# Expert-choice routing: token numbers and gates by fp32r products, scatter matrices at other places

## The reference

```python
def expert_choice_ffn(h, router_w, w_gate, w_up, w_down):
    cap = EC_CAPACITY * n // N_EXPERTS            # 64 latent or 32 context tokens per expert
    aff = jax.nn.softmax((h @ router_w).astype(F32), axis=-1)
    gate, idx = lax.top_k(jnp.swapaxes(aff, 1, 2), cap)
    xe = jax.vmap(lambda hb, ib: hb[ib])(h, idx)
    a = jnp.einsum('becd,edf->becf', xe, w_gate)
    u = jnp.einsum('becd,edf->becf', xe, w_up)
    ye = jnp.einsum('becf,efd->becd', jax.nn.silu(a) * u, w_down) * gate[..., None].astype(h.dtype)
    return ...zeros((n, D)).at[ib.reshape(-1)].add(yb.reshape(-1, D))
```

## Time and profile before

| | us |
|---|---|
| median of 3 runs | 2724.34 (2723.0 to 2728.15) |
| the profiled execution | 2721.45 |
| its span, first to last instruction | 2719.7 |
| mean granted TensorE clock | 0.97 of 2.4 GHz |

### The profile page before, as it was taken

One profiled execution on the slowest core, in us unless ns is written; L12 is line 12 of the kernel. 1 busy time (PEld: TensorE's weight loads), 2 busy tenths in 40 slices (PEclk: granted clock), 3 DMA queues, 4 the chain that ended last, 5 costly groups with the idle time before them and its releaser, 6 DMA issues. The chain is left out here.

```text
span 2719.7 us, 36663 instructions
## 1 busy us (share of the span) xinstructions
PE 2541.3 (93%) x15344; PEld 1580.0 (58%) x15344; DVE 1173.0 (43%) x2219; ACT 773.3 (28%) x1586; POOL 22.7 (1%) x48
## 2 busy tenths in 40 slices
PE   8989999999999999978899999999999968988887
PEld 7856888887677877756433434344767743322222
DVE  5455633333887877875101111113566441111113
ACT  4345433333422222223111111113357421101002
POOL 0000000000000000000000000000000000000000
PEclk9989999999999999987999999999999979999999
DMA  5332322222210111036799999997230278999996
GB/s 199 112 132 80 136 93 95 93 93 80 90 34 32 49 51 61 0 140 264 292 373 357 345 347 349 350 341 279 98 155 2 73 307 359 428 428 427 428 427 274
DMA packets 55100, 562.44 MB, mean 207 GB/s; under 512 B 6511, under 2 KB 14711, under 8 KB 22168
## 3 DMA queue, kind: packets, MB, share of 16 engines
q1 hardware_dynamic: 50616, 544.37, 51.4%
q0 software_dynamic: 2880, 10.49, 1.1%
q10 hardware_dynamic: 1440, 5.24, 0.5%
HBM read 552.74 MB, written 7.34 MB: 206 GB/s over the span
## 5 line engine op out<-in xcount | busy, mean ns | idle before, releaser
L3730 DVE SCALAR_TENSOR_TENSOR residual<-experts_psc,mod,residual 128x512 f32<-128x512 f32 (+1 forms) x102 | 72.8, 718 | 420.5 <-PE experts_psc L3581 353.3
L2914 PE MATMUL moe_gate<-ring,moe_xe_l 128*64 128x512 f32 x728 | 193.3, 609 | 14.4 <-DMA ring<-in_moe_gu 10.4
L2914 PE MATMUL moe_up<-ring,moe_xe_l 128*64 128x512 f32 x728 | 189.0, 597 | 0.0
L3511 PE MATMUL experts_py_l<-ring,experts_turn_l 128*64 128x512 f32 x752 | 170.8, 596 | 12.4 <-DMA ring<-in_moe_down 9.9
L1017 DVE TENSOR_TENSOR mlp_w_lo<-ring,mlp_w_hi 128x512 fp32r<-128x512 f32 x144 | 96.7, 688 | 97.9 <-ACT mlp_w_hi L962 97.6
L3639 ACT ACTIVATE experts_act_l<-moe_gate 128x512 f32<-128x512 f32 x32 | 19.1, 598 | 386.5 <-PE moe_up L2914 386.5
L3715 DVE TENSOR_TENSOR experts_y_low<-experts_py_l,experts_y_whole 64x512 fp32r<-64x512 f32 x64 | 44.1, 689 | 192.3 <-ACT experts_y_whole L3656 170.9
L962 ACT CAST mlp_w_hi<-ring 128x512 fp32r<-128x512 f32 x144 | 86.4, 618 | 123.6 <-PE mlp_acc L918 123.6
L3511 PEld LDWEIGHTS experts_py_l<-ring,experts_turn_l 128*64 128x64 f32 x752 | 51.7, 137 | 116.0 <-issue 98.1
L2914 PEld LDWEIGHTS moe_up<-ring,moe_xe_l 128*64 128x64 f32 x728 | 53.0, 138 | 104.9 <-issue 104.9
L3704 DVE SCALAR_TENSOR_TENSOR experts_hid_l<-experts_act_l,moe_gate_rows,moe_up 128x512 f32<-128x512 f32 x32 | 23.9, 747 | 207.4 <-ACT experts_act_l L3639 207.4
(11 more groups left out here) (602 smaller groups left out, 5268.3 us busy)
## 6 DMA issues: line engine op xcount, KB each, us to landing
ring<-in_moe_gu SPq DMA_DIRECT2D x91, 2048.0 KB, 9.4
ring<-in_moe_down SPq DMA_DIRECT2D x47, 2048.0 KB, 9.1
ring<-in_ada_w SPq DMA_DIRECT2D x24, 2048.0 KB, 7.9
moe_wide_early<-in_moe_gu SPq DMA_DIRECT2D x9, 2048.0 KB, 30.5
moe_wide_low<-in_moe_gu SPq DMA_DIRECT2D x9, 2048.0 KB, 30.5
normed<-in_moe_gu SPq DMA_DIRECT2D x9, 2048.0 KB, 30.5
moe_wide_high<-in_moe_gu SPq DMA_DIRECT2D x9, 2048.0 KB, 30.5
ring<-in_w_up SPq DMA_DIRECT2D x8, 2048.0 KB, 7.8
```

The source lines that it names most:

```text
L2914: last = core.nc.tensor.matmul(banks[m][64 * half:64 * half + 64, :], xe_l[:, e, k, :], columns(2 * kk + m, FH * half, FH), start=(k == 0) ...
L3511: last = nc.tensor.matmul(py_l[64 * half:64 * half + 64, :], turn_l[:, c, i, :], columns(n, c, FH * half, FH), start=(f == 0), stop=(f == ...
L3730: nc.vector.scalar_tensor_tensor(out=x[:, d, c0:c0 + n], in0=banks[bank][:, 0:n], scalar=gate[j][:, d:d + 1], in1=x[:, d, c0:c0 + n], op0= ...
```

## The change

`find` uses fp32r operands. The affinities are split into a part rounded to fp32r and the rest, so that the moving side `facts` has 2 + 2 x 16 = 34 columns (the token number twice, sixteen high parts, sixteen rests) in place of 17. Two small copies on ScalarE make the high parts, two subtractions on VectorE the rests, and GpSimd writes the numbers. The result is copied out of PSUM (`near`), and VectorE adds high part and rest of each gate; ScalarE's gate copies go. In layer 1 the spreads use the two banks of `pr`; TensorE waits for the gates ahead of them. Four are made ahead of the gathers, the other eight one behind each of gathers 0 to 7. In layer 2 the spreads move from behind chunks 5 to 8 to behind chunks 9 to 12, and `rest_of_y(0)` moves on VectorE from chunk 9 to behind them. Core of the diff (the context streams have the same lines with their own sizes):

```diff
@@ route_stage @@
-    F = 1 + E
+    F = 2 + 2 * E
...
-        part = ada.part(st, MOD_OPEN[layer] + MOD_ROUTE[layer], ([pa], pl[:, 256:512]))
+        part = ada.part(st, MOD_OPEN[layer] + MOD_ROUTE[layer], ([pa], pl[:, 448:512]))
...
-        facts = {"l": pl, "c": pr[:, 512:1024]}
+        near = {"l": st.sb("near_l", [P, F * (E // 2)]), "c": st.sb("near_c", [P, F * (E // 4)]) if ctx else None}
+        found_in = {"l": pl, "c": pr[:, 512:1024]}
+        spread_to = [pr[:, 0:512], pr[:, 512:1024]]
...
-        aff = st.sb("aff", [P, LT, 1 + W])
+        aff = st.sb("aff", [P, LT, W])
+        facts = {"l": st.sb("facts_l", [P, LT, F], F32R), "c": st.sb("facts_c", [P, CT, F], F32R) if ctx else None}
@@ gpsimd @@
-                nc.gpsimd.tensor_copy(aff[:, :, 0], number[:, CAP_L:CAP_L + LT])
+                nc.gpsimd.tensor_copy(facts["l"][:, :, 0:2], number[:, CAP_L:CAP_L + LT].unsqueeze(2).to_broadcast([P, LT, 2])).then_inc(numbered.handle, 1)
+                nc.gpsimd.memset(aff[:], 0.0)
@@ tensor @@
-                            last = nc.tensor.matmul(facts[s][:, F * j:F * (j + 1)], src.bitcast(F32).rearrange("p e s -> p (e s)"), aff[:, t, number_at:number_at + F],
+                            last = nc.tensor.matmul(found_in[s][:, F * j:F * (j + 1)], src.rearrange("p e s -> p (e s)"), facts[s][:, t, :],
...
-                find("l", 0, LT, 0)
+                pe.wait_ge(numbered.handle, numbered.at(1))
+                pe.wait_ge(aff_split.handle, aff_split.at(1))
+                find("l", 0, LT)
                 if ctx:
-                    find("c", LT, tiles, C0)
+                    find("c", LT, tiles)
                     part.products(pe, part.n - 1)
-                pe.wait_ge(tok_kept.handle, tok_kept.at(len(halves)))
-                for i, (s, j) in enumerate(scatters):
-                    if i >= 4:
-                        pe.wait_ge(spread_kept[i % 2].handle, spread_kept[i % 2].at((i - 4) // 2 + 1))
+
+                def spread_rows(i):
+                    s, j = scatters[i]
+                    if i >= 2:
+                        pe.wait_ge(spread_kept[i % 2].handle, spread_kept[i % 2].at(i // 2))
...
+                if ctx:
+                    pe.wait_ge(gates_kept.handle, gates_kept.at(2))
+                    for i in range(4):
+                        spread_rows(i)
+                    part.turn(pe, part.n - 1)
+                pe.wait_ge(tok_kept.handle, tok_kept.at(len(halves)))
                 for j in range(len(groups)):
                     gather(j)
+                    if ctx and j < 8:
+                        spread_rows(4 + j)
@@ scalar @@
+                act.wait_ge(softmaxed.handle, softmaxed.at(1))
+                if ctx:
+                    nc.scalar.copy(facts["c"][:, :, 2:2 + E], aff[:, 0:CT, C0:C0 + E])
+                nc.scalar.copy(facts["l"][:, :, 2:2 + E], aff[:, :, 0:E]).then_inc(aff_high.handle, 1)
...
-                act.wait_ge(indexed.handle, indexed.at(1))
-                for odd in range(2):
-                    for half in range(2):
-                        nc.scalar.copy(gate_rows[64 * half:64 * half + 64, :].rearrange("p (j o) -> p o j", o=2)[:, odd, :],
...
@@ vector @@
+                def gates(dst, s, rows, first, step, n):
+                    high, low = (near[s][rows, at:at + step * (n - 1) + 1:step] for at in (2 + first, 2 + E + first))
+                    return nc.vector.scalar_tensor_tensor(out=dst, in0=high, scalar=1.0, in1=low, op0=ALU.mult, op1=ALU.add)
...
+                dve.wait_ge(aff_high.handle, aff_high.at(1))
+                if ctx:
+                    nc.vector.tensor_tensor(facts["c"][:, :, 2 + E:F], aff[:, 0:CT, C0:C0 + E], facts["c"][:, :, 2:2 + E], ALU.subtract)
+                nc.vector.tensor_tensor(facts["l"][:, :, 2 + E:F], aff[:, :, 0:E], facts["l"][:, :, 2:2 + E], ALU.subtract).then_inc(aff_split.handle, 1)
...
+                link(nc.vector.tensor_copy(near["l"][:], pl[:, 0:F * (E // 2)]))
+                for odd in range(2):
+                    for half in range(2):
+                        last = gates(gate_rows[64 * half:64 * half + 64, :].rearrange("p (j o) -> p o j", o=2)[:, odd, :],
+                                     "l", slice(64 * odd, 64 * odd + 64), odd, F + 2, E // 2)
+                last.then_inc(gates_kept.handle, 1)
@@ experts_stage @@
-        SPREAD_FROM = WideRing.ROWS
+        SPREAD_FROM = at["down", 0, DOWN_CHUNKS - 1]
+        rest_at = {at["down", e, DOWN_CHUNKS - 1]: e for e in range(0 if ctx else 1, E)}
+        if not ctx:
+            rest_at[SPREAD_FROM + E // 4 - 1] = 0
...
-                    if what == "down" and i == DOWN_CHUNKS - 1:
-                        rest_of_y(e)
+                    if n in rest_at:
+                        rest_of_y(rest_at[n])
```

More of the change, by code:

```diff
@@ L3038, in turn_half, with find @@
                     last.then_inc(tok_turned.handle, 1)
-                def find(s, first, last_tile, number_at):
+                def find(s, first, last_tile):
                     n = E // 2 if s == "l" else E // 4
@@ L3249, in _ @@
                 if ctx:
+                    keep_spread(1)
+                    keep_spread(3)
                     part.keep_columns(dve)
```

47 lines of the change are left out of this document (25 added, 22 removed).

## The result

The changed kernel takes 2708.96 us (median of 5, 2704.34 to 2711.91) beside 2724.34: ratio 0.9942, 95% interval 0.9931 to 0.9953, which is 15.4 us less. Timed once more, beside a kernel before of 2722.57 us, it took 2706.25: ratio 0.9937 (0.9924 to 0.9951), 16.3 us less. Forecast were 19.8.

What follows compares the result with a forecast made beforehand. The find products were taken to be on the path in both layers, ahead of TensorE-bound and DMA-bound experts. Savings of 9.4 + 6.4 + 4.0 = 19.8 us from the 2724.34 median gave 2704.5 us, range 2697 to 2712.

Steps and rivals of the forecast that it cites:

- the finds: Routing of both layers: fp32r find products at 0.216 us take 6.9 us instead of 13.84, 6.9 us less per layer.
- forecast case: Whole kernel: all predicted savings arrive, 19.8 us less, 2704.5 us; own span 2701 to 2708; chance 50%.
- B: Layer 1: TensorE runs interleaved gathers and spreads at half clock, 4.9 us earlier instead of 9.4; 2709 us; chance 12%.
- D: Layer 2: the weight stream pauses elsewhere and the moved spreads give nothing; 2708.5 us; chance 8%.
- Rival C: Finds: narrow fp32r products cost 0.33 us each, so 7 us of the saving are missing; 2711.5 us; chance 8%.
- rival A: Finds: the fp32r weight load is half as long; 2701 us, or 2697.5 with a raised clock; chance 17%.
- F: Finds do not shorten and moved spreads give nothing; only 2.5 us from layer 1's gathers remains; 2722 us; chance 3%.
- The work added on ScalarE and VectorE: Both routings: affinity copies, subtractions and gates moved to VectorE cost zero; 0.4 us if the subtractions' cover were gone.
- Layer 1 behind the find: Layer 1's row gathers, sharing DMA with one expert chunk, end 9.4 us earlier; bounds 6.9 and 10.6.
- Layer 2, the first gather: Layer 2's gathers start 6.4 us earlier, after 0.5 off for sharing with weight loads; bounds 5.6 and 6.9.
- Layer 2's spreads: Layer 2's experts: moving spreads behind chunks 9 to 12 issues chunk 16 earlier, 4.0 us less; bounds 0 and 4.1.
- rival E: Layer 2: down(1) at chunk 14 lacks its turned copy or rest, making the kernel slower; 2732 us; chance 2%.

Runs made afterwards that it cites:

- fp32 run: Changed kernel, but with find products reading the same 34 columns and pick matrices as fp32: 2715.78 us, ratio 0.9978.
- second trace: Changed kernel once more, unaltered: 2706.25 us, ratio 0.9937 against the kernel before.
- The run with an even faster find: Dummy products ahead of both layers' finds, against the changed kernel with layer 1's spreads all ahead of the gathers: 2706.77 us, ratio 0.9952.
- first trace: Profile of the changed kernel as first measured: 2708.96 us, ratio 0.9942 against the kernel before.

## Why the prediction held, and which of its terms were too large

2704.5 us was forecast with a range of 2697 to 2712; 2708.96 and 2706.25 lie in it, the first 1 us beyond the forecast case's own span (2701 to 2708). It is not luck that carried the sum: the largest term, the finds, was right, and the others were all too large, none made up for another. But two rivals name about the same time, B 2709 and D 2708.5, and only the traces and the kernels with single parts tell them from the forecast case.

**The finds: right.** 32 and 8 products at 0.216 us and a clock of 0.50, the first cast 6.8 us nearer to the first pick (8.4 against 15.2) in both layers, forecast 6.9; the context 1.7, forecast 1.8. Rival C (0.33 us a product) and rival A (a shorter load) are out: the load is the same 333 ns at the lower clock in the fp32r and the fp32 run, and only their number halves. So is F (no shorter find). The work added on ScalarE and VectorE cost nothing, as said: TensorE's chain from the picks to the first gather is 11.2 us shorter, forecast 11.5.

**Layer 1 behind the find: the mis-sized step.** I priced the gathers and the chunk as one heap of DMA work, 24.7 us at a share of 0.95, and let its sum set the end; 9.4 us in all (1306.4 less 1297.1 is 9.3, a slip of 0.1). P1 to X1 fell by 6.2 and 7.9 us. Both are below the forecast, and the first is below its bound of 6.9. The heap has about the right size (0.74 of 31.55 us and 0.77 of 29.9, 23 us, over the same stretch in the two traces), but its order matters: the chunk is issued 0.4 us behind group 3, group 3 lands with it some 12 us after its issue (11.8 in the second trace), TensorE turns the groups in order, and the DMA engines then run empty for 3 us because no buffer is free. In the kernel before the chunk came 2 us behind group 3 (1282.12 and 1280.04), the group landed after 6.1 us, and twelve spreads stood ahead. Moving eight of these behind the gathers, which I counted as a pure gain, took the cover off that wait; with them ahead, P1 to X1 falls by 9.2 us (two traces; 10.5 in a third), near the forecast's number by other means. That the clock would fall in the interleaved stretch was rival B; it did, to 0.50 from 1282 to 1288, but after the 5 us of idling, not by the interleaving, since with the chunk held to twelve groups it is 1.00 from 1273 to 1293. The stretch from 1282 to 1295 that the prediction set against B was not of transposes alone, as it says: eight products of the modulation turn stood in it, at 1283.79. The new traces have cleaner ones. On that rule of the Trainium skill ("TensorE: Matmul & The Clock Gate", PE-mode transpose), by which transposes don't bring the full clock, the trace disagrees again: only transposes ran from 1283.87 on, and those at 1288.62 took 1.08 us for eight.

**Experts of layer 1 pass the gain on whole: right**, within a scatter of up to 4.7 us between executions.

**Layer 2, the first gather: short.** Forecast 6.4 with bounds 5.6 and 6.9; P2 to G2 fell by 5.4 and 5.0, below the lower bound. Of 6.8 us won by the find, 1.4 to 1.8 went to rows that are used later after their issue, where I had taken off 0.5. The table shows a limit: counted from R2, the first gather comes at 45.1 to 45.9 us in nine of the ten traces with the routing's find in fp32r and no dummies ahead of it, whether the first pick came at 29.6 or 30.7; only the finds alone, with the pick at 32.0, reach 46.2 and have the 6.5 us less from P2 to G2 that were forecast. The run with an even faster find won 2.2 us more and waited 2.5 more than its base. While TensorE waits for these rows, the DMA share is 1.00 (2219.5 to 2225.5 in the first trace) and 0.98 in the second, where in the kernel before the DMA engines had nothing else to do when these rows were issued (0.02 from 2226.3 to 2231). That the rows wait behind the last weight loads fits this, but no run moved the loads.

**Layer 2's spreads: half.** Chunk 16 came 3.1 to 3.7 us earlier behind the first gather than in the kernel before, and 4.6 earlier than with the finds alone; forecast 4.1. Down(1) of chunk 14 was not late, so rival E is out. The end followed by 1.1 to 2.9 us in the traces; the timed pairs give 3.5 (1.1 to 5.7) and 2.9, so D, nothing at all, is out too, but the size is not settled between 1 and 4. The formula "issue plus all that follows" took the latest chunk and a stream without loss behind it. By my own numbers chunks 14 and 16 to 20 ended within 1.1 us of each other (2683.5 to 2684.6), so that there was little reserve behind the latest; and W to end is 425.3 to 426.3 in every kernel with the moved spreads, 423.8 and 424.6 without.

Sum, from the second trace, in the order of the table: 0.6 ahead of the change, 6.8 + 1.1 in layer 1, nothing between, 6.8 less 1.8 in P2 to G2, 3.3 less 1.5 at chunk 16 and behind: 15.3, the difference of the spans. Against the 19.8 forecast, layer 1 lacks 1.5 us, layer 2's rows 1.4 and its spreads 2.2, and 0.6 came from ahead of the change. In layer 1 it was the mechanism that was wrong, not only a size: not the sum of the DMA work set the end but one group that landed late; the range covered what that cost (1.5 to 3.2 us).

## What to carry to other kernels

A small DMA that others wait for should not be issued just ahead of a large one: here it landed over 5 us later with 0.4 us between them, and on time with 1.7. Ask of every step that is shortened which transfer is now issued next to which, not only how much work the engines have. Work that stands ahead of a wait may be its cover; before it is moved, price the wait without it. And where a stream is fed just in time by several steps in a row, moving the latest may only uncover the next. Time the parts of a change singly: here one of three gave as much as the whole.

## What the runs showed of the hardware

- Half a megabyte of rows by indirect DMA (128 rows) landed 10.9 to 11.9 us after its issue in layer 1 when a 2 MB chunk was issued from 0.6 us before it to 1.0 us behind it. With the chunk 1.7 to 2.1 us behind, it was 6.1 to 6.5; rows issued 4.4 to 7 us behind a chunk landed after 6.3 to 6.4 us in the kernel with fp32 products, but after 7.9 to 8.6 behind the delayed group 3 of the changed kernel; the other rows of layer 1 took 4.2 to 6.4. In layer 2, with chunks issued 5.5 us apart, the last three groups took 7.6 to 15.3.
- An fp32 product of 128 weight columns and 17 or 34 moving ones is two weight loads and two records 0.216 us apart at the 1.2 GHz level, an fp32r product with 34 is one of each. The moving columns don't show in that spacing (13.84 us for 32 fp32 products with 17 and with 34), only in the length of a record (375 and 406 ns).
- A weight load of 128 columns lasts 333 ns in the finds at the lower clock level, in fp32 and in fp32r; 189 to 192 ns at the full one.
- The granted clock fell from 1.00 (1254 to 1257) over 0.89 to 0.50 (1261 to 1264) during the find with dummies ahead, TensorE having been busy 3.92 of 4 us and then 3.00 of 3. In the changed kernel it rose from 0.50 to 1.00 while only transposes of 128 columns ran: eight took 1.97 us at 1283.87, 1.91 at 1286.49 and 1.08 at 1288.62.
